# The v products of two tokens at a time in the periods with late products

## The reference

```python
# c: (tokens, 1024); s1, s2: the 16 best of 128 sub-keys per head, 8 heads
best_s, pos = lax.top_k(cand_s, PEER_TOPK)            # 16 of 256 per head -> 128 experts a token
gates = jax.nn.softmax(best_s, axis=-1)
u = jnp.take(u_tab, ib, axis=0)                       # 128 rows of 1024 for each token
coef = gb * jax.nn.gelu(jnp.einsum('cd,ced->ce', xb, u), approximate=False)
return jnp.einsum('ce,ced->cd', coef, jnp.take(v_tab, ib, axis=0))   # 128 rows again
```

## Time and profile before

| | |
|---|---|
| median of three runs | 3401.3 us |
| profiled execution, own time | 3405.59 us |
| its span, first to last instruction | 3403.9 us |
| PE, DVE, POOL busy, share of span | 80%, 70%, 58% |
| slots 140 to 447 | 582 to 1567 us, 985 us, 3.20 us a slot |
| in them: PE, DVE, POOL busy | 875, 714, 591 us |
| granted TensorE clock there | 0.95 |
| moved by DMA there | 368.69 MB, 374 GB/s |
| period 4, slots 512 to 639 (1748.6 to 2103.7 us) | 405 GB/s, clock 0.83 |

### The profile page before, as it was taken

How to read it: one execution, slowest core, us unless ns; L and a number is a source line. 1 busy time by engine, 2 the same in 40 slices (tenths; PEclk the granted TensorE clock), 3 DMA queues, 4 the chain that set the end, 5 groups by cost and what they waited for, 6 DMA issues and landing times.

```text
span 3403.9 us, 41995 instructions
## 1 busy us (share of the span) xinstructions
PE 2719.1 (80%) x15556; PEld 1235.5 (36%) x15556; DVE 2378.7 (70%) x6051; ACT 525.0 (15%) x1166; POOL 1978.4 (58%) x2093
## 2 busy tenths in 40 slices
PE   9988985998989888897867687667766777777787
PEld 7877872333323233233323233232323331222111
DVE  5669898886677765777689877987798747665200
ACT  3221321110121101211010101010111001111101
POOL 1013344665656565566677667776767667666663
PEclk9998996998999999998878887798879788888899
DMA  6558998999999999999999999999999999999995
GB/s 212 197 181 301 334 364 286 373 399 380 371 352 385 390 364 362 340 406 390 410 409 403 405 401 409 397 407 405 400 396 408 406 404 410 409 388 406 410 369 235
DMA packets 385725, 1248.57 MB, mean 367 GB/s; under 512 B 40560, under 2 KB 75120, under 8 KB 384752
## 3 DMA queue, kind: packets, MB, share of 16 engines
q0 software_dynamic: 294912, 1073.87, 81.0%
q1 hardware_dynamic: 90608, 172.01, 14.1%
HBM read 1217.80 MB, written 27.92 MB: 366 GB/s over the span
## 4 chain that ended last, share of the span: by engine, by line
PE 34%; DMA 33%; DVE 16%; POOL 10%; issue 5%; ACT 1%; SPq 1%; POOLq 0%; ACTq 0%; DVEq 0%
DMA e_u<-in_u_tab,e_idx 12%; PE e_acc L1273 8%; DMA e_late<-in_u_tab,e_idx 7%; DMA e_v<-in_v_tab,e_idxT 6%; DVE e_u L2178 5%; PE e_pl L1361 5%; POOL e_v L949 4%; PE e_pd L1156 4%; POOL e_u L941 3%; PE e_acc L1318 3%; PE e_pd L1236 3%; PE e_acc L1343 3%; DVE e_late L2178 2%; PE e_pd L976 2%; DMA shifted_projection<-e_side 2%
## 5 line engine op out<-in xcount | busy, mean ns | idle before, releaser
L2178 DVE CUSTOM_DVE_ANT_0 e_u<-e_u,e_c 128x1024 f32<-128x1024 f32 x776 | 943.3, 1216 | 439.8 <-DMA e_u<-in_u_tab,e_idx 424.4
L941 POOL DMA_INDIRECT e_u<-in_u_tab,e_idx x776 | 757.7, 976 | 651.4 <-DVE e_dots L2178 260.2
L1273 PE MATMUL e_acc<-e_v,e_wd 128*32 128x512 f32 x3096 | 900.5, 675 | 284.5 <-DMA e_v<-in_v_tab,e_idxT 260.6
L949 POOL DMA_INDIRECT e_v<-in_v_tab,e_idxT x774 | 732.8, 947 | 434.7 <-PE e_acc L1273 279.2
L2178 DVE CUSTOM_DVE_ANT_0 e_late<-e_late,e_c 128x1024 f32<-128x1024 f32 x248 | 301.1, 1215 | 132.3 <-DMA e_late<-in_u_tab,e_idx 130.5
L1273 PEld LDWEIGHTS e_acc<-e_v,e_wd 128*32 128x32 f32 x3096 | 122.7, 113 | 736.6 <-DMA e_v<-in_v_tab,e_idxT 493.1
L1361 PE MATMUL e_pl<-e_late,e_v 128*128 128x512 f32 x608 | 342.0, 661 | 54.6 <-DVE e_late L1977 13.5
L1273 PE MATMUL e_acc<-e_late,e_wd 128*32 128x512 f32 x832 | 270.8, 712 | 105.0 <-DMA e_late<-in_v_tab,e_idxT 96.1
L941 POOL DMA_INDIRECT e_late<-in_u_tab,e_idx x248 | 240.5, 970 | 189.8 <-DVE e_dots L2178 148.9
L1906 DVE SCALAR_TENSOR_TENSOR e_gbc<-e_hc,e_cw,e_gbc 128x128 f32<-128x128 f32 x960 | 303.7, 343 | 0.5
L949 POOL DMA_INDIRECT e_late<-in_v_tab,e_idxT x208 | 198.2, 953 | 75.2 <-issue 53.1
(11 more groups left out here) (293 smaller groups left out, 3048.2 us busy)
## 6 DMA issues: line engine op xcount, KB each, us to landing
e_u<-in_w_in SPq DMA_DIRECT2D x38, 512.0 KB, 3.8
e_v<-in_w_in SPq DMA_DIRECT2D x38, 512.0 KB, 6.5
e_v<-in_w_in SPq DMA_DIRECT2D x76, 256.0 KB, 6.4
e_u<-in_u_tab,e_idx POOLq DMA_INDIRECT x776, 9.5
e_v<-in_v_tab,e_idxT POOLq DMA_INDIRECT x774, 9.5
e_zb<-in_w_c SPq DMA_DIRECT2D x48, 256.0 KB, 10.5
e_arena<-in_w_r SPq DMA_DIRECT2D x32, 256.0 KB, 19.8
e_zb<-in_w_r SPq DMA_DIRECT2D x32, 256.0 KB, 6.7
```

The source lines that it names most:

```text
L941: pool.indirect_dma_start(out=rows_in[i], out_offset=None, in_=io["u_tab"], in_offset=bass.IndirectOffsetOnAxis(ap=idx[n % 2][:, j:j + 1], ...
L949: pool.indirect_dma_start(out=rows_in[i], out_offset=None, in_=io["v_tab"], in_offset=bass.IndirectOffsetOnAxis(ap=idxT[n % (LAG + 1)][:, ...
L1273: last = pe.matmul(acc[rows, cols], w[:, at_:at_ + 32], rows_in[row][:, cols], start=(step == 0), stop=True, skip_group_check=True)
L2178: dve.tensor_tensor_reduce(rows_in[i], rows_in[i], c[:, :], 1.0, 0.0, ALU.mult, ALU.add, dots[n % 2][:, j:j + 1]).then_inc(s_dot, 1)
```

## The change: pairs, in every second slot

While t < 8 and g < 448 TensorE does nothing for v in an even slot, and in the odd slot behind it takes two tokens, j - 1 and j: left half of both, then right half of both. From slot 448 on it is one token a slot as before, and four a time from t = 8. The gathers, their order and all else stay.

```diff
-TOGETHER, LAST_TOGETHER = 1, 4
+LAST_TOGETHER = 4
...
-                    together = LAST_TOGETHER if t >= NT else TOGETHER
-                    if v_at(t, s) and s % together == 0:
-                        add_tokens(*v_at(t, s), together)
+                    if v_at(t, s):
+                        n, j = v_at(t, s)
+                        if t >= NT:
+                            if s % LAST_TOGETHER == 0:
+                                add_tokens(n, j, LAST_TOGETHER)
+                        elif t * SLOTS + s >= MORE_AT:
+                            add_tokens(n, j, 1)
+                        elif s % 2:
+                            add_tokens(n, j - 1, 2)
```

## The result

The changed kernel takes 3426.1 us (median of 6 runs, 3418.6 to 3431.3), the kernel before beside it 3399.1 us: ratio 1.0075, interval 1.0057 to 1.0094. It is slower by 26 us (27 by the medians). I had forecast 3381 us and a range up to 3422, with 0.24 for slower; the prediction was wrong in sign and in range. The number lies nearest the slower rival, which I had put at 3419; how much of that rival came true stands further down.

A forecast was written before the change was run, and what follows sets the result against it. Over slots 140 to 447 it took TensorE mostly as the bound, the DMA close behind; stretch terms summed to -20 us, 3405.6 to 3385.6, less 4.3 for the profiled run's excess over the median: 3381 us, range 3350 to 3422.

The forecast's parts named there:

- the slower rival: Recurrences and slots behind them: loop and buffers decide, +31 us there, +18 us overall, 3419 us; chance 0.24 including no overlap.
- output mixing: Twice 8 slots where the output is mixed: 25.5 us each would become about 22, together -7 us.
- the six slots behind it: Six slots after output mixing, twice, one late product a slot: relief against the DMA limit leaves -2 us, by judgement.
- the slots with two late products: Only late tiles starting on an odd slot save 0.98 us each, some five in periods 1 and 3: -5 us.
- the first ten slots of periods 2 and 3: Twenty slots with one product a slot, at most 0.47 us each, a little under half taken: -4 us.
- recurrences and what follows them: Three recurrences of 24 slots -3, 0, -3 us; following 22 slots +1 each in two of them: together -4 us.
- The pair's cost, 1.00 us: On TensorE, two tokens ordered left, left, right, right take 1.00 us, within bounds of 1.00 and 1.98.
- The relief, 145 us: TensorE below slot 448: 148 groups of 0.98 us less, 145 us of its time, 0.47 us a slot.
- The rival of the clock: A less busy TensorE gets a lower clock, +106 us of its time; only 5 us gained, 3396 us; chance 0.14.
- The store's chain: Next store waits for the tile's first half: 11.4 + 0.7 us + two slots of products; even-started tiles save nothing.
- The loop through VectorE: Even-slot u gather behind the pair of slot g - 3: 14.6 us for four slots, 3.6 a slot where it closes.
- The refill of the v buffers, 2.8 us: GpSimd issues the pair's second v gather 2.8 us after release; at 7.7 us landing, 2.9 us a slot.

The follow-up runs named there:

- relief alone: Kernel before, with v products below slot 448 covering 256 of 512 columns of each half, releases one by one: 3381.5 us, ratio 0.9954.
- The release in pairs alone: Kernel before, only GpSimd changed: below slot 448 an even-slot token's v gather waits until the next odd slot's token is done too: 3440.6 us, ratio 1.0125.
- the eleventh kernel: Kernel before, one token a slot, with the u gather ahead of the v gather in each slot below 448: 3580.4 us, ratio 1.0018, slower chip.
- u, v, v, u: Changed kernel with GpSimd's gathers below slot 448 ordered u, v, v in even slots and u in odd: 3388.7 us, ratio 0.9973, first chip.

## Why the prediction was wrong, point by point

The terms of the sum in us, forecast and measured (from the table by slots): output mixing -7 and +4.1; the six slots behind it -2 and -2.6; the slots with two late products -5 and +1.4; the first ten slots of periods 2 and 3 -4 and +5.1; recurrences and what follows them -4 and +13.6; mixer and query products +2 and +3.0. Together -20 and +24.6.

- **What bounds the kernel.** Right in kind: TensorE was a bound, and relief alone brings 16 us.
- **The pair's cost, 1.00 us.** Right where both rows have landed: 1045.55 to 1046.55. Often the second had not, and the 1.00 leaves that out: 1276.09 to 1278.11, 2.02 us. Of the 154 pairs of the region 54 start all eight matmuls within 0.6 us; of the 308 single tokens before, 292 do so with their four.
- **The relief, 145 us.** Right in TensorE's list, but it shows as 59 us less of busy time (816 against 875), and as 76 us in the v products' own matmuls, since pairs now often start with one row landed and wait for the other with matmuls open, and since the granted clock fell from 0.95 to 0.92. The rival of the clock so had a true part, a small one: the kernel with the relief alone has the same 0.92 and is faster.
- **The store's chain in the slots with two late products.** I had forecast nothing for the tiles with an even start in period 2 and got -2.8 us there, -2.1 in period 1; 10 to 19 lost 6.3 us together, where I counted a gain. All the slots with two late products together give +1.4 (6.3 - 4.9), where I had forecast -5.
- **Output mixing, -7.** Measured +4.1. In period 2 two of its four pairs waited for their second row: one took 2.02 us (1276.09 to 1278.11), one 3.22 us (1281.81 to 1285.03), where I had 1.0. That the buffers' 2.5 us and GpSimd's 2.5 us lie at the same place, I had written; I took them side by side, and they stand in one queue.
- **The loop through VectorE.** This is the step that failed. Its price of 3.6 us a slot where it closes no run isolates (the changed recurrences took 3.2 to 3.4 a slot on the whole), but I gave it too few slots: "one step in six slots; in the other slots TensorE runs on". TensorE doesn't run on: late tiles wait for ScalarE and VectorE (59 us, 32 before), pairs wait for v rows (67.8 us, 43.8 before), dot products wait for u in 213 places instead of 176, and after one long wait GpSimd's list comes in a burst, a gather each 1.25 us. The release in pairs alone, with no relief to set against it, cost 1.25%, where the sum had almost nothing for it. In the recurrences and behind them (s 20 to 65) I had -4 us and got +13.6, which is 18 of the 45 us between forecast and result; the other 27 lie in stretches to which I gave no loop at all. That the rival's 3419 is so near is in part luck: it had +31 in the recurrences and behind them, 5 more lost in the DMA-bound stretches and -18 outside, and the slots show +13.6 there and +11.0 in all the rest.
- **"Landing shortens when fewer gathers are out."** It did, by about 1 us (mean of v gathers in s 44 to 65: 8.0 to 7.0, 7.3 to 6.8, 8.2 to 7.0 us, from issue to landing), and that was too little against a release later by a slot of 2.9 us. Behind a burst it can be longer, as the 10.62 us above.
- **The refill of the v buffers, 2.8 us.** A smaller cost: making it 1.55 us with u first brings 0.002 on the first chip, within the intervals.

What stays open: why pairs cost 1.1% when the second token is taken early, and why no order mends them, on the slower chip. Its DMA moves less (below), which may tie both loops tighter; how long gathers take to land there its traces don't tell, since about half of the landings' marks are missing in them, and no run changed landing alone. Open too is what the order of the gathers brings without pairs on the first chip.

## What to carry to other kernels

When one engine's instructions release buffers for a queue, taking two at once moves work on that engine, but also makes every request behind the first release late. Price what stands behind that wait on the queue (here the u gathers, which have nothing to do with the v buffers) before the relief: on the first chip coupling the releases cost 39 us by the medians (42 by the ratio) by itself, the relief gave 16 to 20. If such a pair is wanted, first put the requests that don't need the release ahead of it on the queue; on the first chip that took the loss away, on the slower one it didn't.

## What the runs showed of the hardware

- Two kinds of chip: a window of the periods after the late products, one token a slot in both, moves 405 GB/s on the first and 364 on the slower (the eleventh kernel):

```profile
1850.00:2250.00 400.00, 255.51 (x1654) 117.00 (x1653) 288.72 (x744) 43.98 (x101) 250.19 (x261) 0.76 0.97 364
```

  The same edit (u, v, v, u) is 0.9973 on one and 1.0132 on the other, and the intervals (0.9959 to 0.9986, 1.0107 to 1.0157) lie far apart: ratios of this kernel from chips of the two kinds can't be compared. Whether the slower chip is slower by itself, or something beside the kernel took part of its memory's rate, no run shows.
- Two tokens with the halves in the order left, left, right, right take 1.00 us, as long as two in the order left, right, left, right.
